# A two-block transformer kernel: x's squares from feature tiles, the first weight units in halves, c times h in one step, and a narrow block packed to 128 columns

## The reference

```python
def _rmsnorm(x, w):
    x32 = x.astype(jnp.float32)
    y = x32 * lax.rsqrt(jnp.mean(x32 * x32, axis=-1, keepdims=True) + EPS)
    return (y * w.astype(jnp.float32)).astype(x.dtype)

def first_block(x, ...):
    h = _rmsnorm(x, attn_norm_w[l])
    proj = jnp.einsum('bsd,de->bse', h, w_in[l])
    q_pre, fz_f, fz_b, i_pre, gate, b_gate, c_gate, h_conv = jnp.split(proj, SPLIT_OFFSETS, axis=-1)
    y_rec = _hgrn2_mixer(q_pre, fz_f, fz_b, i_pre, gate, lbs_f[l], lbs_b[l], hgrn_norm_w[l])
    y_conv = _short_conv_mixer(b_gate, c_gate, h_conv, conv_w[l])   # b * conv(c * h)
    x = x + concat(y_rec, y_conv) @ w_out[l]
    h2 = _rmsnorm(x, ffn_norm_w[l]) ; x = x + (silu(g) * u) @ w_down[l]
    return _rmsnorm(x, final_norm_w)

def _layer(x, c_act, pos, ...):          # the second block
    ada = (c_act @ w_ada + b_ada)[:, None, :]
    h = _rms(x, g_norm1) * (1 + sc1) + sh1
    proj = h @ w_in
    c_q, c_kv, k_pe, q_sb, k_sb, v_sb, gl_a, gl_b = jnp.split(proj, ...)   # k_pe: 64 columns
    ...                                  # two kinds of attention, gated and merged
    x = x + gt1 * (merged @ w_out)
    h2 = _rms(x, g_norm2) * (1 + sc2) + sh2
    x = x + gt2 * ((silu(gate) * up) @ w_ffn_out)
```

## Time and profile before

| | |
|---|---|
| median of three runs | 2475.89 us |
| the profiled execution's own time | 2476.12 us |
| its span, first to last instruction | 2474.3 us |
| PE busy | 2466.5 us (100%) |
| DVE busy | 1748.3 us (71%) |
| ACT busy | 1194.0 us (48%) |
| DMA, mean over the span | 235 GB/s, 582.37 MB |

### The profile page before, as it was taken

How to read it: one execution, slowest core, us unless ns; L and a number is a source line. 1 busy time by engine, 2 the same in 40 slices (tenths; PEclk the granted TensorE clock), 3 DMA queues, 4 the chain that set the end, 5 groups by cost and what they waited for, 6 DMA issues and landing times.

```text
span 2474.3 us, 29559 instructions
## 1 busy us (share of the span) xinstructions
PE 2466.5 (100%) x11904; PEld 2169.2 (88%) x11904; DVE 1748.3 (71%) x2154; ACT 1194.0 (48%) x1469; POOL 26.9 (1%) x27
## 2 busy tenths in 40 slices
PE   9999999999999999999999999999999999999999
PEld 8898898888888888888888888888888888888888
DVE  6887798788888788886665565466788765555555
ACT  6544544544444444445765554444644444444443
POOL 0000000000000000000010000000000000000000
PEclk9999999999999999999999999999999999999999
DMA  8656666788888888887455455555588756555554
GB/s 335 237 190 235 223 206 249 259 306 306 291 302 307 305 293 298 303 295 250 160 187 173 156 171 195 202 193 187 187 291 301 279 188 205 202 201 204 190 203 151
DMA packets 82632, 582.37 MB, mean 235 GB/s; under 512 B 9409, under 2 KB 9793, under 8 KB 12609
## 3 DMA queue, kind: packets, MB, share of 16 engines
q1 hardware_dynamic: 82352, 580.38, 66.5%
q10 hardware_dynamic: 144, 0.12, 0.0%
HBM read 578.36 MB, written 2.10 MB: 235 GB/s over the span
## 4 chain that ended last, share of the span: by engine, by line
PE 98%; DMA 0%; DVE 0%; ACT 0%; SPq 0%; issue 0%; POOL 0%; ACTq 0%
PE bank L851 31%; PE bank L852 31%; PE bank L853 31%; PE bank L561 3%; PE bank L641 1%; DMA raw<-in_w_in_dram 0%; PE bank L679 0%; PE bank L690 0%; PE bank L691 0%; PE bank L660 0%; PE bank L649 0%; PE bank L659 0%; PE bank L680 0%; PE bank L702 0%; SPq L1970 0%
## 5 line engine op out<-in xcount | busy, mean ns | idle before, releaser
L1275 DVE TENSOR_TENSOR wlo<-raw,whi 128x1024 fp32r<-128x1024 f32 x886 | 1080.2, 1223 | 631.2 <-ACT whi L882 626.6
L882 ACT CAST whi<-raw 128x1024 fp32r<-128x1024 f32 x886 | 928.1, 1049 | 917.0 <-PE bank L853 882.2
L851 PE MATMUL bank<-whi,hH 128*128 128x512 f32 x2528 | 972.1, 385 | 0.3 <-DVE wlo L1275 0.2
L852 PE MATMUL bank<-wlo,hH 128*128 128x512 f32 x2528 | 960.0, 380 | 0.0
L853 PE MATMUL bank<-whi,hL 128*128 128x512 f32 x2528 | 959.8, 380 | 0.0
L853 PEld LDWEIGHTS bank<-whi,hL 128*128 128x128 f32 x2528 | 479.2, 190 | 67.1
L851 PEld LDWEIGHTS bank<-whi,hH 128*128 128x128 f32 x2528 | 479.3, 190 | 66.3 <-issue 1.2
L852 PEld LDWEIGHTS bank<-wlo,hH 128*128 128x128 f32 x2528 | 479.4, 190 | 64.3
L1702 DVE SCALAR_TENSOR_TENSOR adacc<-raw,stat,adacc 128x512 f32<-128x512 f32 x360 | 269.8, 749 | 6.8
L851 PE MATMUL bank<-whi,aH 128*128 128x512 f32 x704 | 267.7, 380 | 0.0
L852 PE MATMUL bank<-wlo,aH 128*128 128x512 f32 x704 | 267.2, 379 | 0.0
(11 more groups left out here) (294 smaller groups left out, 1420.3 us busy)
## 6 DMA issues: line engine op xcount, KB each, us to landing
raw<-in_w_gu_dram SPq DMA_DIRECT2D x176, 1024.0 KB, 5.0
raw<-in_w_ada_dram SPq DMA_DIRECT2D x96, 1024.0 KB, 5.3
raw<-in_w_down_dram SPq DMA_DIRECT2D x88, 1024.0 KB, 4.9
raw<-in_w_in_dram SPq DMA_DIRECT2D x62, 1024.0 KB, 4.8
raw<-in_w_in2b_dram SPq DMA_DIRECT2D x56, 1024.0 KB, 4.8
raw<-in_w_out_dram SPq DMA_DIRECT2D x32, 1024.0 KB, 4.8
raw<-in_w_in2a_dram SPq DMA_DIRECT2D x8, 1024.0 KB, 4.8
raw<-in_w_mla_dram SPq DMA_DIRECT2D x8, 1024.0 KB, 4.8
```

Of the source, the lines that this page charges most:

```text
L851: e.matmul(o, xh[:, kt, sl], pairs(wh, i), start=k == 0, stop=False)
L852: e.matmul(o, xh[:, kt, sl], pairs(wl, i), start=False, stop=False)
L882: e.copy(whi[i][:, :, :], raw[u % RAW][:, 2 * hf:2 * hf + 2, :]).then_inc(*ev("act_hi", c, 0))
L1275: e.tensor_tensor(wlo[i][:, :, :], raw[u % RAW][:, 2 * hf:2 * hf + 2, :], f(whi[i][:, :, :]), ALU.subtract).then_inc(*ev("dve_lo", c, 0))
```

## The change

- The squares of x are made by ACT from the xT tiles in SBUF, in eight operations of 512 columns in slots 5 to 8, without a sum. DVE adds the eight tiles up in slots 7 to 9 (seven adds, and one of 256 columns). PE sums over the partitions with two one-column products in slot 11, DVE copies these to r1's columns and makes the mean. The two loads of x0 are gone. Block 0's side work comes one slot earlier (5 instead of 6). The Exp and Sigmoid of the small vectors move from slot 5 to 10, and what DVE makes of them from slot 6 to 11.
- SP loads the units 1, 2 and 3 in halves, xT in seven pieces (kt 8-9 and 10-11 apart), ident before unit 5, and positions and frequencies before unit 12.
- The warm-up has 14 products of 512 columns instead of 30 of 128. A tiny ACT Copy ahead of the wait for vec makes ACT load its table then.
- c is not transposed: ACT evacuates it as before, and DVE multiplies it with h, scaled by r1, as it evacuates h at t = 0; PE transposes the product in h's turn, and ACT copies it to U.
- In the narrow block ACT and DVE write high and low parts side by side, 64 and 64 columns for each feature tile. PE does 32 products of 256 columns with 128-column weights, into 128 partitions: both parts by high, both parts by low activations. The two transposes are full ones, and DVE adds the two halves of the result, before ACT squares it.

```diff
-WARM = 30
+WARM = 14
...
-XT_AT = (0, 2, 4, 6, 8, 12, 16)
+XT_AT = (0, 2, 4, 6, 8, 10, 12, 16)
...
+        def narrow(t, side_by_side, lo):
+
+            if not side_by_side:
+                return t.rearrange("p (k n) -> p k n", n=64)
+            return t.rearrange("p a b -> p (a b)").rearrange("p (k h n) -> p k h n", h=2, n=64)[:, :, lo, :]
+
+        SQ = T + AD[:1]
...
-            return 6 if b.index == 0 else 0
+            return 5 if b.index == 0 else 0
...
-        EVT = ("q", "c", "h", "b")
+        EVT = ("q", "h", "b")
...
-                        ins = turn(o[:, 64 * m:64 * m + 64], ev_tmp(b, 0)[0:64, P * m:P * m + P], 64)
+                        ins = turn(o[:, P * m:P * m + P], ev_tmp(b, 0)[:, P * m:P * m + P])
...
+                if s == 11:
+                    e.wait_ge(*on("dve_x0", "halves"))
+                    o = next_bank(e, "x0")
+                    for m in range(2):
+                        ins = e.matmul(o[:, m:m + 1], SQ[0][:, P * m:P * m + P], f(ones_r[:, 0:1]), start=True, stop=True)
+                    ins.then_inc(*ev("pe_x0"))
...
-                    wh = wh[:, :, :].rearrange("p a b -> p (a b)").rearrange("p (k n) -> p k n", k=KT)
-                    wl = wl[:, :, :].rearrange("p a b -> p (a b)").rearrange("p (k n) -> p k n", k=KT)
-                    o = acc(b, 0)[0:64, 0:S]
+                    o = acc(b, 0)[:, 0:S]
                     if pl.acc_n[b.index, 0]:
                         e.wait_ge(sem_acc[2 * (b.index % 2)], pl.acc_n[b.index, 0])
                     for kt in range(KT):
-                        e.matmul(o, wh[:, kt, :], xh[:, kt, :], start=kt == 0, stop=False)
-                        e.matmul(o, wl[:, kt, :], xh[:, kt, :], start=False, stop=False)
-                        ins = e.matmul(o, wh[:, kt, :], xl[:, kt, :], start=False, stop=kt == KT - 1)
+                        both = (wh, wl)[kt // 8][:, :, :].rearrange("p a b -> p (a b)")[:, P * (kt % 8):P * (kt % 8) + P]
+                        e.matmul(o, both, xh[:, kt, :], start=kt == 0, stop=False)
+                        ins = e.matmul(o, both, xl[:, kt, :], start=False, stop=kt == KT - 1)
...
-                e.matmul(banks[7][:, 0:P], ones_r[:, :], ones_r[:, :], start=True, stop=True)
+                e.matmul(banks[7][:, :], ones_r[:, :], ones_r[:, :].unsqueeze(1).to_broadcast([P, 4, P]), start=True,
+                         stop=True)
...
+                if b.kind == "kpe":
+                    for k, w in enumerate((whi, wlo)):
+                        e.copy(narrow(w[i][:, :, :], True, 0), narrow(raw[u % RAW][:, k, :], False, 0)).then_inc(
+                            *ev("act_hi", c, k))
+                    return
...
-                elif kind in ("q", "c") and t == 2:
+                elif kind in ("q", "h") and t == 2:
...
-                elif kind == "kpe" and t == 1:
-                    e.wait_ge(*on("pe_turn", b.index))
-                    for m in range(2):
-                        ins = e.activation(ev_tmp(b, 1)[:, 64 * m:64 * m + 64], side(b.index)[:, 64 * m:64 * m + 64],
+                    e.copy(ev_tmp(b, 0)[:, 0:S], acc(b, 0)[:, 0:S]).then_inc(*acc_free(b, 0))
+                elif kind == "kpe" and t == 2:
+                    e.wait_ge(*side_read(b.index))
+                    for m in range(2):
+                        ins = e.activation(ev_tmp(b, 1)[:, 64 * m:64 * m + 64], ev_tmp(b, 1)[:, S + 64 * m:S + 64 * m + 64],
...
-                if 9 <= s < 13:
-                    m, q = (s - 9) // 2, (s - 9) % 2
-                    if q == 0:
-                        e.wait_ge(sem_x0[m], 16)
-                    for j in (2 * q, 2 * q + 1):
-                        ins = e.activation((T + AD[1:])[4 * m + j][:, :], x0[:, m, 512 * j:512 * j + 512], ACT.Square, bias=0.0,
-                                           scale=1.0, accum_out=sc(ssq + 4 * m + j))
-                    if s == 12:
-                        ins.then_inc(*ev("act_x0"))
-                if s == 5:
+                if 5 <= s < 9:
+                    for i in (2 * s - 10, 2 * s - 9):
+                        e.activation(SQ[i][:, :], xT[:, 2 * i:2 * i + 2, :].rearrange("p a b -> p (a b)"), ACT.Square,
+                                     bias=0.0, scale=1.0).then_inc(*ev("act_x0", i))
+                if s == 10:
...
+            e.wait_ge(*on("dve_half"))
+            e.activation(sc(b_warm), sc(b_half), ACT.Copy, bias=0.0, scale=1.0)
...
+            def squares_of_x(s):
+
+                def add(o, i, name):
+                    e.tensor_tensor(o, o, i, ALU.add).then_inc(*ev("dve_x0", name))
+
+                if s == 7:
+                    e.wait_ge(*on("act_x0", 1))
+                    add(SQ[0][:, :], SQ[1][:, :], "0+1")
+                    e.wait_ge(*on("act_x0", 3))
+                    add(SQ[2][:, :], SQ[3][:, :], "2+3")
+                elif s == 8:
+                    e.wait_ge(*on("dve_x0", "2+3"))
+                    add(SQ[0][:, :], SQ[2][:, :], "0..3")
+                    e.wait_ge(*on("act_x0", 5))
+                    add(SQ[4][:, :], SQ[5][:, :], "4+5")
+                elif s == 9:
+                    e.wait_ge(*on("act_x0", 7))
+                    add(SQ[6][:, :], SQ[7][:, :], "6+7")
+                    e.wait_ge(*on("dve_x0", "6+7"))
+                    add(SQ[4][:, :], SQ[6][:, :], "4..7")
+                    e.wait_ge(*on("dve_x0", "4..7"))
+                    add(SQ[0][:, :], SQ[4][:, :], "all")
+                    e.wait_ge(*on("dve_x0", "all"))
+                    add(SQ[0][:, 0:S], SQ[0][:, S:2 * S], "halves")
+                elif s == 11:
+                    e.wait_ge(*on("pe_x0"))
+                    e.tensor_copy(sc(b_r1, 2), side("x0")[:, 0:2]).then_inc(*side_free("x0"))
+                    e.wait_ge(*side_read("x0"))
...
-                elif kind == "h" and t == 2:
-                    for m in range(2):
-                        d = U[:, :, 1 + P * m:1 + P * m + P]
-                        e.wait_ge(*on("pe_turn", b.index, m))
-                        if m == 0:
-                            c = pl.at["c", b.arg[0]].index
-                            e.wait_ge(*side_read(c, 0))
-                            e.wait_ge(*side_read(c, 1))
-                        e.tensor_tensor(d, v4(side(b.index, m)), d, ALU.mult).then_inc(*side_free(b.index, m))
+                elif kind == "h" and t == 0:
+                    c = pl.at["c", b.arg[0]]
+                    e.wait_ge(*visit(end))
+                    for m in range(2):
+                        e.wait_ge(*acc_read(c, m))
+                        e.scalar_tensor_tensor(plain(ev_tmp(b, m)[:, :]), summed(b, m), sc(b_r1 + m),
+                                               plain(ev_tmp(c, m)[:, :]), ALU.mult, ALU.mult).then_inc(*acc_free(b, m))
...
+                elif kind == "kpe" and t == 1:
+                    o = side(b.index)[:, 0:S].rearrange("p (a h b) -> p a h b", a=2, h=2)
+                    d = ev_tmp(b, 1)[:, S:S + P].rearrange("p (a b) -> p a b", a=2)
+                    e.wait_ge(*on("pe_turn", b.index))
+                    e.tensor_copy(d, o[:, :, 0, :]).then_inc(*ev("dve_kpe", "high"))
+                    e.wait_ge(*on("dve_kpe", "high"))
+                    e.tensor_tensor(d, o[:, :, 1, :], d, ALU.add).then_inc(*side_free(b.index))
...
-                if u == 3:
-                    load_xT(5)
+                if u == 5:
+                    e.dma_start(ident[:, :], a["ident"]).then_inc(sem_ident, 16)
+                elif u == 12:
                     e.dma_start(posi[:, :], a["pos"]).then_inc(sem_pos, 16)
                     e.dma_start(freq[:, :], a["freq"].partition_broadcast(P)).then_inc(sem_pos, 16)
-                elif u in (5, 7):
-                    m = (u - 5) // 2
-                    e.dma_start(x0[:, m, :], a["x"][:, m, :]).then_inc(sem_x0[m], 16)
-                    if u == 7:
-                        e.dma_start(ident[:, :], a["ident"]).then_inc(sem_ident, 16)
...
-                if u < 2:
-                    for i in range(2 - u):
-                        sl = slice(512 * i, 512 * i + 512 * (u + 1))
-                        e.dma_start(dst[:, sl], a[name][k][:, sl]).then_inc(sem_first[2 * u + i], 16)
-                    load_xT(1 + 2 * u)
+                if u < 4:
+                    if u == 0:
+                        for i in range(2):
+                            sl = slice(512 * i, 512 * i + 512)
+                            e.dma_start(dst[:, sl], a[name][k][:, sl]).then_inc(sem_first[i], 16)
+                    else:
+                        e.dma_start(dst[:, 0:1024], a[name][k][:, 0:1024]).then_inc(sem_first[u + 1], 16)
+                    if u < 3:
+                        load_xT(1 + 2 * u)
                     e.dma_start(dst[:, 1024:2048], a[name][k][:, 1024:2048]).then_inc(sem_raw[u], 16)
-                    load_xT(2 + 2 * u)
+                    if u < 3:
+                        load_xT(2 + 2 * u)
```

(46 more changed lines are left out.)

4 lines of the change are left out of this document (2 added, 2 removed).

## The result

The changed kernel takes 2471.67 us, median of 20 runs (2471.27 to 2472.19); the kernel before took 2475.89 in 20 runs beside it (2475.21 to 2476.61). The ratio is 0.9983, 95% interval 0.9976 to 0.999. That is 4.2 us less, 0.17%, inside the range of 2470.4 to 2474.8 and 0.3 us from the predicted 2472.0. The profiled execution took 2471.29 us, its span 2469.5, against 2474.3 before: 4.8 us less, because it is one of the quicker ones. Part of this document is about that spread.

The account below looks back on a forecast made before the run. PE was taken as the bound, busy for all but 8 us of the span. Terms -0.58 - 1.74 - 1.82 - 0.2 + 0.44 = -3.9 us, from the median 2475.89 to 2472.0; range 2470.4 to 2474.8.

Parts of the forecast that it names:

- Bound: Whole kernel: one microsecond of PE work removed is one microsecond gained, wherever no operand is late.
- c and h: Two c blocks: eight transposes fewer in each, -1.74 us; the moved evacuations and multiplication on ACT and DVE cost nothing.
- Narrow block: Narrow block's products on PE: 32 instead of 48 at an unchanged pitch of 0.1138, -1.82 us (-2.0 to 0).
- Rival (b): Narrow block: wider weight loads not hidden, pitch 0.171, no gain from the products; sum -2.1, 2473.8 us; chance 0.07.
- The transposes: Narrow block's two transposes, full instead of 64 partitions: -0.2 us (-0.25 to 0).
- Sums of squares: PE ahead of chunk 11: two one-column f32 products, four passes, +0.44 us (0.2 to 0.7), DVE's adds hidden.
- Start: First chunks: chunk 4 starts at 19.46 instead of 20.04 through the new load order, -0.58 us.
- worth nothing of their own: First chunks: early table load and warm clock gain nothing, since chunk 2's late operand covers them.
- rival (a): Start: unit 1's half lands earlier than 11.9, chunk 4 at 18.2; sum -5.1, 2470.8 us; chance 0.11.
- Whatever PE did before 20.04 is forgotten: Start of the kernel before: chunk 4 waited 0.38 us for its operand, so PE's earlier pace did not count.
- (c): Start: transfers in halves change nothing, as many smaller transfers use up the saving; sum -3.3, 2472.6 us; chance 0.08.
- (d): First chunks: PE's idle gaps drop the clock or delay its rise, making it slower; rise at 36 gives 2482.8; chance 0.03.

Follow-up runs that it names:

- the two single parts: Kernel before with only the edit of c and h, 2474.68 us; kernel before with only the edit of the narrow block, 2474.53 us.
- the second profile: Profiled execution of the changed kernel run again with no edit, chunk 4 starting at 19.44; median 2471.54 us over 11 runs.

## Why the prediction was right, and the step that was not

**Bound.** PE's work counts one for one. Right: 3.16 us of PE's terms came out of the span: from chunk 4 on the changed kernel is shorter by 3.2 (3.17 between the two profiles), and neither of the two single parts brought a new wait. The total is nearer than its terms: the start gave 0.5 to 0.9 more than forecast, by the medians, and the narrow block 0.2 less. That these partly cancel is luck.

**c and h.** -1.74 predicted, -1.74 in the traces (0.87 at each of the two blocks), -1.6 in the run of that part alone. The covers named (casts three chunks ahead) held.

**Narrow block.** -1.82 predicted, -1.62 measured: the pitch is 0.120 and not 0.1138. Rival (b), the wider load paid in full, would have been 0.171. The Trainium skill (TensorE: Matmul & The Clock Gate, "LDWEIGHTS (loading the stationary operand)") puts a load at its columns divided by 1.2, in ns, which is 53, 80 and 107. The traces agree that it grows with the columns and by how much, about 30 ns for 32 of them, but show 133, 161 and 192 ns. Of the 58 ns between 64 and 128 columns a product pays 6. The transposes gave 0.24 for 0.2.

**Sums of squares.** +0.44 predicted and measured in the trace; this part was not run alone. DVE's last add was predicted for 36.4 with PE at 37.6, and came at 34.57 with PE at 36.51.

**Start.** The sum's -0.58 fits an execution in which unit 1's half lands at 11.7, as the second profile shows (-0.60), and is 1.1 us too small for the first. Typical by the medians is -1.1 to -1.5, so this term was sized at about half or less. The step that failed is the sentence that the early table load and the warm clock are "worth nothing of their own, since the late operand of chunk 2 covers them". The text named the way out of it (if the half lands earlier) and gave it 0.11 as rival (a), but it is the ordinary case: in the fourteen profiles the half landed between 10.6 and 11.9, and the profile before, whose landing was taken over, had the latest of them all. With the warm-up and the table load undone it is PE's slow chunk 0 that holds the start, and 0.9 to 1.3 us of the gain is lost. Undoing the table load alone cost nothing; undoing the warm-up alone cost 0.2 to 0.6.

The sentence failed by the prediction's own numbers too, if by little. Its chunk 1 starts at 11.05. With the old warm-up chunk 0 ended at 11.89 in the profile before, and chunks run on from there start chunk 4 at 19.66 and not at 19.46.

Behind that is an error of reading. "Whatever PE did before 20.04 is forgotten" was true of one profile, with 0.38 us to spare. In all five other runs with the old warm-up chunk 4 started without a wait, at 20.05 and 20.58 with unit 2 loaded whole (clock up at 11.8 and 12.7), at 19.12, 19.32 and 19.41 with it in halves (9.9, 10.2 and 10.3): the later the clock came up, the later chunk 4. The start of the kernel before had two bounds within half a microsecond of each other, and a single profile showed one.

**Rivals.** (c) is out by the traces: with unit 2 whole and the new warm-up chunk 4 waits for it, and with unit 2 in halves no kernel waits there. The order alone gave 0.7 by the medians, in a trace whose clock also came up early. (d) is out: the clock was up before the first real product in the changed kernel, and gaps of 1 us before chunks 1 and 2 (0.8 and 0.9 us of waiting in the second profile) did not bring the lower level back; the products behind them have a pitch of 0.22. The warm-up of 512-column products took 5.4 us, less than 14 x 0.427 = 6.0, so the clock rose within it.

## What to carry to other kernels

Where an engine's wait for an operand is shorter than what changes from run to run, the profile shows one of two bounds, and the other has to be priced as well: here the start's second bound stood 0.4 us behind the first, and an edit judged worthless against the first gave up to a microsecond. When a transfer's arrival sets the pace, cut the path behind it (cast, subtraction, first use) into smaller pieces too; that gave 0.6 to 0.7 us on top of the smaller transfers. Where a kernel's time less the start of one chunk is constant, its scatter lies ahead of that chunk, and medians can be turned into starts. And look at the starts of the products behind a warm-up: it has done its work only if they are already at the short pitch.

## What the runs showed of the hardware

The clock. Behind 6.5 us of 128-column products (1.08 to 7.55) it rose only after 512-column ones had begun at 7.55, and not always alike: at 11.0 in the profile before, and between 9.9 and 12.7 in five others of these runs. Behind 512-column products on ones from 1.08 on it rose before 6.6 us in both profiles of the changed kernel; with the new warm-up alone it came up only near 6.7, as the 14 products ended. The Trainium skill (TensorE: Matmul & The Clock Gate, "What's actually happening") says that activity releases the throttle; the runs agree, and show that 128-column products, each behind a weight load of its own, did not do it in 6.5 us.

The first transfers. The same half unit landed at 11.9, 10.7 and 11.7 us in three executions. In the two slower ones the transfers ran at 247 and 250 GB/s between 8 and 10 us, in the quicker one at 273, with the DMA engines 91 to 101% busy, against 415 to 436 from 12 to 14 us. Over all fourteen traces the rate from 8 to 10 us is 245 to 326 GB/s, and it goes with the landing only roughly (251 with 11.0, 286 with 11.1). Three stretches of the second profile of the changed kernel; the last numbers of a line are the granted clock, the DMA share and GB/s:

```profile
6.00:8.00 2.00, 1.47 (x7) 1.14 (x7) 2.00 (x5) 1.68 (x4) 0.00 (x0) 1.00 1.03 383
8.00:10.00 2.00, 1.59 (x8) 1.05 (x6) 1.34 (x3) 1.86 (x3) 0.00 (x0) 1.00 0.98 250
...
12.00:14.00 2.00, 1.26 (x6) 0.76 (x4) 1.12 (x1) 1.88 (x4) 0.00 (x0) 1.00 1.05 422
```

Issuing the half unit a microsecond sooner left its landing in the same range, in one trace. What slows the transfers there stays open, and whether it is the order in memory of the half units wasn't tried.
